# Splitting and multiplying the second index-query unit ahead of the memory rows

## The reference, cut to what matters

```python
h = rmsnorm(x, g_pre[i])
(gq, gk, gv, ga, gz, dq, dk, dv, iq, ik, iw, dz, xq, xz, gates) = split_cols(h @ w_in[i])
y_dsa = dsa_mixer(dq, dk, dv, iq, ik, iw, dz, rel_bias)
y_mem = cross_mixer(xq, xz, rmsnorm(mem, g_mem[i]), w_mem_kv[i])
...
# in dsa_mixer: the index scores that choose the keys
s = jax.nn.relu(jnp.einsum('bqhd,bsd->bqhs', iqb.astype(jnp.float32), ik_f))
score = jnp.einsum('bqhs,bqh->bqs', s, iwb.astype(jnp.float32))
...
# in cross_mixer: keys and values of the memory rows
mk, mv = jnp.split(mem_n @ w_mem_kv, 2, axis=-1)
```

## Time and profile before

| | us |
|---|---|
| median of 3 executions | 907.86 |
| lowest and highest | 907.37 and 908.78 |
| span of the profiled execution, first to last instruction | 906.1 |
| TensorE busy in that span | 887.1 (98%) |
| VectorE busy | 574.6 (63%) |
| ScalarE busy | 438.6 (48%) |
| GpSimd busy | 53.5 (6%) |

### The profile page before, as it was taken

How to read it: one execution, slowest core, us unless ns; L and a number is a source line. 1 busy time by engine, 2 the same in 40 slices (tenths; PEclk the granted TensorE clock), 3 DMA queues, 4 the chain that set the end, 5 groups by cost and what they waited for, 6 DMA issues and landing times.

```text
span 906.1 us, 14153 instructions
## 1 busy us (share of the span) xinstructions
PE 887.1 (98%) x5792; PEld 766.9 (85%) x5792; DVE 574.6 (63%) x880; ACT 438.6 (48%) x644; POOL 53.5 (6%) x79
## 2 busy tenths in 40 slices
PE   8999999999999999999989999899999999999996
PEld 6888999898999888888779999677888788888885
DVE  4975664574647665655569977654377667777543
ACT  6744444744344544444356524663444555555441
POOL 1000000000020110000110141100000100000000
PEclk9999999999999999999999999999999999999998
DMA  9657643455445545555656655004565555555441
GB/s 304 218 186 218 223 147 133 139 186 186 136 149 181 187 148 177 166 189 187 225 188 152 175 123 204 3 2 140 140 232 182 167 186 186 186 186 186 163 163 47
DMA packets 127799, 151.70 MB, mean 167 GB/s; under 512 B 16967, under 2 KB 93126, under 8 KB 127734
## 3 DMA queue, kind: packets, MB, share of 16 engines
q1 hardware_dynamic: 127594, 150.70, 51.9%
q0 software_dynamic: 64, 0.07, 0.0%
q10 hardware_dynamic: 76, 0.02, 0.0%
HBM read 148.67 MB, written 3.68 MB: 168 GB/s over the span
## 4 chain that ended last, share of the span: by engine, by line
PE 86%; DVE 7%; ACT 3%; issue 1%; DMA 1%; SPq 1%; POOL 1%; POOLq 0%; DVEq 0%; ACTq 0%
PE bank L513 17%; PE bank L515 17%; PE bank L514 17%; PE bank L1250 9%; PE bank L539 5%; PE bank L1238 5%; PE bank L540 2%; DVE w_lo L1954 2%; DVE arena L2331 1%; DMA arena<-in_mem 1%; ACT w_hi L1426 1%; PE bank L720 1%; PE bank L700 1%; PE bank L819 1%; PE bank L939 1%
## 5 line engine op out<-in xcount | busy, mean ns | idle before, releaser
L1954 DVE TENSOR_TENSOR w_lo<-ring,w_hi 128x2048 fp32r<-128x2048 f32 (+1 forms) x134 | 300.6, 2249 | 142.9 <-ACT w_hi L1426 142.2
L1426 ACT ACTIVATE w_hi<-ring 128x2048 fp32r<-128x2048 f32 (+1 forms) x134 | 250.3, 1871 | 129.4 <-PE bank L515 85.2
L513 PE MATMUL bank<-h_both,w_hi 128*128 128x256 f32 x496 | 143.1, 289 | 2.0 <-DVE w_lo L1954 2.0
L514 PE MATMUL bank<-h_both,w_hi 128*128 128x256 f32 x496 | 140.3, 283 | 0.0
L515 PE MATMUL bank<-h_both,w_lo 128*128 128x256 f32 x496 | 140.3, 283 | 0.0
L1250 PE MATMUL bank<-h_both,w_hi 128*128 128x512 f32 x352 | 123.4, 398 | 0.0
L513 PEld LDWEIGHTS bank<-h_both,w_hi 128*128 128x128 f32 x496 | 95.0, 192 | 4.2 <-DVE w_lo L1954 2.7
L1238 PE MATMUL bank<-h_both,w_lo 128*128 128x256 f32 x352 | 97.8, 281 | 0.4 <-ACT h_both L1449 0.4
L514 PEld LDWEIGHTS bank<-h_both,w_hi 128*128 128x128 f32 x496 | 95.1, 192 | 0.6 <-issue 0.5
L515 PEld LDWEIGHTS bank<-h_both,w_lo 128*128 128x128 f32 x496 | 95.1, 192 | 0.0
L513 PE MATMUL bank<-w_hi,h_both 128*128 128x512 f32 (+1 forms) x224 | 86.1, 384 | 0.0
(11 more groups left out here) (343 smaller groups left out, 1477.2 us busy)
## 6 DMA issues: line engine op xcount, KB each, us to landing
ring<-in_w_in SPq DMA_DIRECT2D x59, 1024.0 KB, 5.0
ring<-in_w_gate_up SPq DMA_DIRECT2D x44, 512.0 KB, 4.4
ring<-in_w_down SPq DMA_DIRECT2D x10, 1024.0 KB, 5.0
ring<-in_w_mem_kv SPq DMA_DIRECT2D x8, 1024.0 KB, 7.4
ring<-in_w_in SPq DMA_DIRECT2D x8, 512.0 KB, 5.0
ring<-in_w_gla_out SPq DMA_DIRECT2D x4, 1024.0 KB, 4.9
ring<-in_w_x_out SPq DMA_DIRECT2D x4, 1024.0 KB, 5.1
ring<-in_w_dsa_out SPq DMA_DIRECT2D x4, 1024.0 KB, 5.5
```

Of the source, the lines that this page charges most:

```text
L513: mm(o, ah, bh, start=start, stop=False, skip_group_check=True)
L514: mm(o, ah, bl, start=False, stop=False, skip_group_check=True)
L1426: act(w_hi[:, k % NHI, 0:m], ring[:, order.index(name) % NSLOT, 0:m], ACT.Copy)\
L1954: tt_(w_lo[:, i, 0:m], ring[:, i, 0:m], w_hi[:, k % NHI, 0:m].bitcast(F), ALU.subtract)\
```

## The change

TensorE multiplies `iq1` before it transposes the memory rows. ScalarE copies `small` and makes the high part of `iq1` before it squares the memory rows, and VectorE makes the low part of `iq1` before it scales them. ScalarE then takes the copy of `iq1` out of its bank before it makes the high parts of the memory rows, and some of the combined helper calls are written out so that a split doesn't come earlier than named.

```diff
@@ TensorE
             done("ik2", ins)
+            project_channels("iq1", h_parts)
             transpose_tokens("m", memn)
-            project_channels("iq1", h_parts)
             pe.wait_ge(signal("params1"), 16 * 8)
@@ ScalarE
             highs(3)
+            copy("small", smallT, bank_of("small")[:, 0:256])
+            highs(4)
             for t in range(TT):
                 squares("m", memn, 2, t, (signal("mem_in"), 16))
-            copy("small", smallT, bank_of("small")[:, 0:256])
-            copy("iq0", pair(iq, 0))
-            bank_ready("ik2")
+            sc.wait_ge(*full("iq0"))
+            act(pair(iq, 0), bank_of("iq0")[:, :], ACT.Copy).then_inc(bank_reader("iq0"), 1)
+            sc.wait_ge(*full("ik2"))
             act(ikT[0], bank_of("ik2")[0:64, 0:256], ACT.Copy).then_inc(signal("ik2"), 1)
+            highs(5)
+            sc.wait_ge(*full("iq1"))
+            act(pair(iq, 1), bank_of("iq1")[:, :], ACT.Copy).then_inc(bank_reader("iq1"), 1)
             high_of_transposed("m", m_hi)
-            copy("iq1", pair(iq, 1))
             copy("tb", bias_out, bank_of("tb")[0:DH, 0:383], scale=128 ** 0.5)
@@ VectorE
             low_of_transposed("x", h_lo, h_hi)
-            lows(3)
+            lows(4)
             scale_rows("m", memn, memn, 2)
-            bank_ready("ik2")
+            ve.wait_ge(*full("ik2"))
             ve.wait_ge(signal("ik2"), 1)
             tsc(iw.rearrange("p a b -> p (a b)"), bank_of("ik2")[:, 256:272], IDX_H ** -0.5 * IDX_D ** -0.5, None, ALU.mult)\
                 .then_inc(reader("ik2"), 1)
             ve.wait_ge(*read("ik2"))
+            lows(5)
             low_of_transposed("m", m_lo, m_hi)
             bank_ready("par1")
```

## The result

| | median, us | against the kernel before | interval (95%) |
|---|---|---|---|
| before | 907.62 | | |
| changed | 911.37 | 1.0032 | 1.0021 to 1.0044 |

The changed kernel is 0.32% slower: 2.9 us by the ratio, with 1.9 to 4.0 as its interval (the two medians alone lie 3.75 apart); forecast were 0.31% and 910.7. The span of its profiled execution is 909.8 against 906.1.

The account below looks back on a forecast made before the run. TensorE, busy 98% of the span, was taken as the bound. The median 907.86 plus 1.26 (later `mk0`: 1.32 gained, 2.58 newly waited) plus 1.58 (clock fall) gave 910.7, chance 0.54; range 908.5 to 911.6.

Parts of the forecast that it names:

- The gain: TensorE's opening: the 1.07 wait before `iq1` goes and running on saves more, so TensorE is ready for `mk0` 1.32 sooner.
- The delay: Later transposes delay splits and the `par1` copy to 36.15; `mk0` waits about 2.5 and starts 1.26 later.
- `mk2` in time: VectorE's low part of `mk2` ends at 47.03, 0.37 before TensorE reaches that unit at 47.40, so no wait.
- The clock: The wait of about 2.5 ahead of `mk0` likelier than not halves the granted clock, costing 1.58.
- Rival A: At `mk0`: the wait alone, clock holding; 1.26 slower, 909.1, chance 0.32.
- its own sign: Prediction wrong if the clock stays at 1.00 through `mk0`; expected was 0.50 for some three microseconds there.
- the rule quoted in the prediction: Trainium skill: throttled clock is the default and only activity lifts it, so `mk0` starts at half rate; sum 910.7.
- Rival B: Ahead of `mk0`: the chain behind the transposes isn't last to end, so all 1.32 stays; 906.5, chance 0.10.
- C: Split of `iq1` not ready at 21.78, so TensorE waits before `iq1` and `mk0`; about 911.7, chance 0.04.

Follow-up runs that it names:

- e1: Changed kernel with VectorE's copy of `par1` taken ahead of the split of `mk1`; 909.71 us, ratio 1.0013 to the kernel before.
- e7: Changed kernel with the `par1` copy ahead of the split of `mk1`, and the split of `mk2` earlier on ScalarE and VectorE; 907.34 us, ratio 0.9990.
- e3: Changed kernel with two products of no use (four long matmuls) put into TensorE's wait ahead of `mk0`; 910.45 us, ratio 1.0020.
- e5: Changed kernel measured once more, unaltered; 911.31 us, ratio 1.0028 to the kernel before.
- e6: Changed kernel with `iq1` still multiplied early but its split back behind the memory rows' squares and scaling; 914.89 us, ratio 1.0069.
- e4_mk1_in_the_gap: Changed kernel with the split of `mk1` moved into ScalarE's and VectorE's idle time ahead of the memory rows' chain; 909.08 us, ratio 1.0003.
- e2_split_early_only: Changed kernel keeping only the early split of `iq1`, with TensorE's order and ScalarE's copy order as before; ratio 0.9993 to the kernel before.
- e8: The kernel of e2_split_early_only measured once more, unaltered; ratio 0.9995 to the kernel before.

## Why the prediction was right, point by point

- **The gain.** Expected 1.32 at the index scores' end. The 1.07 went, as said; TensorE reached the start of the scores 1.30 sooner (30.99 less 0.72, against 31.57), but the scores then took 3.92 in place of 3.44. Each bank of scores is one of the memory rows' banks, which VectorE's low parts empty up to 33.74 (30.51 + 3.23), and I had costed that at 0 to 0.2. It was 0.48. It cost nothing in the changed kernel, since the larger wait hid it, as the prediction said it would; where that wait is gone (e1, e7) it is what keeps the gain at 0.7 and not at 1.3.
- **The delay.** Expected `mk0` 1.26 later, measured 1.53 and 1.54. The links came as named. The extra is in small terms: `iq1` took 5.86 and not 5.76, since its first matmul is slow even with no wait ahead, which left the end of the copy 0.06 late (36.93 less 0.72, against 36.15), and `mk0` started 0.26 after that end (36.93 to 37.19), where I had allowed 0.05. The wait itself was 2.27 and not 2.5, since the scores ended later.
- **`mk2` in time.** It was: no wait there in the changed kernel. VectorE's low part of `mk2` ended at 47.08 (45.51 + 2.29 less 0.72), where 47.03 was forecast. The half rate isn't needed for that: in e3, without it, TensorE starts `mk2` at 48.21, 0.76 after the split's end. In e1 TensorE is there earlier by the wait and the half rate, and VectorE hardly, so a wait of 1.29 comes.
- **The clock.** Expected 1.58 and likelier than not. It fell in both profiles of the changed kernel; 1.55 in the second, and 1.81 in the first, which also holds a slower pace later (below). Against e3, which has the same slower pace, the first comes to 1.41. e3 takes the half rate away without moving the start of `mk0`. But the prediction let the fall come or not come for the kernel as a whole, and the times of e5 show that it comes in some executions only. With it an execution costs the forecast, without it about Rival A; those without it go against the prediction by its own sign, a clock that stays at 1.00 through `mk0`. Nor does `mk0` start at half rate each time, as the rule quoted in the prediction would have it: in e5's profile its first matmul lasts 0.47, at full clock. The median lies at the forecast only because over half of the executions had the fall; nothing in the prediction said that they would, so that is in part luck. So is the size of 1.58, which was read at a place where the fall costs far less in the end (last section).
- **Rival A**, the wait without the clock, is what e3 comes near, and four executions of e5: 1.8 and about 1.6 us, where A gave 1.26. **Rival B** (no wait) and **C** (split not ready) fell on the rows: the wait is there, and `iq1` starts with none.

The sum was 2.84, the measured ratio gives 2.9, the second measurement 2.5; by the medians alone 3.75 and 3.39.

## What to carry to other kernels

A unit of work moved ahead of another delays all that hangs on the other: follow that chain to its last consumer on every engine before counting the wait removed as gain. Here the transposes fed three engines, and the consumer that mattered was a 0.23 copy standing in a queue behind a split of 2.29 that it has nothing to do with. A wait on TensorE is to be priced with the clock behind it: here the start of `mk0` was 1.5 late, and the half-rate matmuls cost as much again (1.41 to 1.55) in the executions in which the clock fell.

## What the hardware showed that I had not expected

Waits of nearly one length don't act alike. In the ten profiles the wait of 2.56 to 2.58 ahead of the second layer's transposes was followed by the low clock in seven and not in three. The changed kernel's own profile is one of the three:

```profile
459.00:460.00 1.00, 0.00 (x0) 0.00 (x0) 0.30 (x1) 0.97 (x3) 0.90 (x2) 1.00 0.00 0
...
461.00:462.00 1.00, 1.00 (x8) 0.82 (x8) 0.36 (x1) 0.00 (x0) 0.94 (x2) 1.00 1.00 340
```

The four waits of 2.25 to 2.28 (`mk0` in two profiles, `iq1` and `mk0` in e6) were all followed by it. Waits far shorter can be, too. In the opening, where TensorE waits several times within a few microseconds, the clock fell in two profiles of ten: in e4_mk1_in_the_gap behind waits of 1.55 and 0.27, and in e2_split_early_only behind waits of 0.57, 0.45 and 0.43 (timeline of TensorE, then clock):

```profile
7.47 1.09 PE L640 MATMUL bank<-arena 128*128 128x128 f32 x8 [0.45 <-DVE arena L1985]
8.99 1.80 PE L640 MATMUL bank<-arena 128*128 128x128 f32 x8 [0.43 <-DVE arena L1985]
```

```profile
8.00:9.00 1.00, 0.57 (x7) 0.34 (x5) 0.81 (x2) 0.06 (x1) 0.15 (x1) 1.00 0.99 270
...
10.00:11.00 1.00, 0.80 (x4) 0.39 (x2) 0.97 (x1) 1.00 (x4) 0.00 (x0) 0.50 1.05 374
```

Eight transposes take 1.09 and the next eight, of the same shape, 1.80, and that profile's L659 is at 22.20 against 20.99, of which 0.53 was there at the first product of `small` already (11.31 against 10.78). Around 580, with waits of 0.4 to 0.8 close together, it fell in five of ten. So an execution has from none (e7) to four (e6) such falls while TensorE still has matmuls to do (behind the last of them the clock falls in all ten), and where differs; that is one likely source of the spread of 1 to 3 us between executions of one kernel, which keeps e2, e7 and e8 from being told apart from the kernel before. What decides in a given execution isn't settled here. The change adds one more place, where it fell in both profiles and, by the times of e5, not in every execution.

Ahead of the second layer the fall costs less than at `mk0`: from the first matmul of line 627 (products of no use that the kernel already runs there) to the next unit it takes 13.17 in the kernel before with the fall and 12.68 in the changed one without, 0.49; in the other profiles it is 12.93 to 13.17 with the fall and 12.67 to 12.69 without. Without the fall the next two steps wait 0.40 for VectorE and 0.42 for ScalarE; with it one of them or both are gone. The price of 1.58 that I took from that row fits `mk0`, where matmuls follow matmuls without such waits.

In some profiles the matmul pairs of `mk0` to `mk3` start 0.353 apart, in others 0.347, with the granted clock at 1.00 in both. Over the 64 pairs that is about 0.4 and explains the rest in e3 (22.69 from `mk0` to `mv0` against 22.29). Its cause is open.
